# Expert outputs weighted on their way out of PSUM and added to the residual in memory by accumulating scatters

## The reference, cut to what matters

```python
h = h + mix
h = h + hierarchical_moe(rms_norm(h, ffn_norm[i]), ...)
...
# in hierarchical_moe: 32 experts, 2 for each token
weights = g_p * e_p / jnp.sum(e_p, axis=-1, keepdims=True)
return (jax.nn.silu(xb @ w_gate[e]) * (xb @ w_up[e])) @ w_down[e]
y = jax.ops.segment_sum(y_buf[dest] * sw[:, None].astype(y_buf.dtype), st, num_segments=T)
...
return rms_norm(h, final_norm)[:, N_META:]
```

## Time and profile before

| | |
|---|---|
| Time, 3 runs | 3458.29 us median (3456.8 to 3461.87) |
| The profiled execution: its own time, its span | 3462.14 us, 3460.2 us |
| Mean granted TensorE clock | 0.952 |
| PE, DVE, ACT, POOL busy | 3136.4, 1756.7, 1247.0, 1798.2 us |
| Moved by DMA | 536.24 MB, 155 GB/s in the mean |
| Expert stages | about 870 to 1365 and 2860 to 3380 us |
| Projection of layer 1 | about 1371 to 1650 us |
| Last stage | about 3384 to 3460.2 us |

### The profile page before, as it was taken

One profiled execution on the slowest core, in us unless ns is written; L12 is line 12 of the kernel. 1 busy time (PEld: TensorE's weight loads), 2 busy tenths in 40 slices (PEclk: granted clock), 3 DMA queues, 4 the chain that ended last, 5 costly groups with the idle time before them and its releaser, 6 DMA issues. The chain is left out here.

```text
span 3460.2 us, 57020 instructions
## 1 busy us (share of the span) xinstructions
PE 3136.4 (91%) x19621; PEld 2480.0 (72%) x19621; DVE 1756.7 (51%) x4064; ACT 1247.0 (36%) x2675; POOL 1798.2 (52%) x1447
## 2 busy tenths in 40 slices
PE   6999999899699996899799999999997996999990
PEld 4788886687688885799566666666665885888880
DVE  3555555577343332666455555555543663433337
ACT  2444444322122222444344444444443221232222
POOL 2655554244344442345588888888872222444433
PEclk8999999899799998899799999999998997999995
DMA  2001100844788893787502220222004546999957
GB/s 103 27 27 40 40 31 28 261 150 136 259 299 303 304 316 119 240 268 237 150 10 53 53 53 10 53 53 53 10 13 173 183 139 224 347 307 321 308 200 298
DMA packets 360887, 536.24 MB, mean 155 GB/s; under 512 B 82934, under 2 KB 280970, under 8 KB 354169
## 3 DMA queue, kind: packets, MB, share of 16 engines
q1 hardware_dynamic: 333624, 457.43, 41.3%
q0 software_dynamic: 27072, 76.40, 5.7%
HBM read 397.42 MB, written 145.06 MB: 157 GB/s over the span
## 5 line engine op out<-in xcount | busy, mean ns | idle before, releaser
L2148 POOL TENSOR_TENSOR ab_acc<-ab_acc,ab_pT 128x1024 f32<-128x1024 f32 (+2 forms) x320 | 593.9, 1856 | 91.9 <-ACT ab_pT L2182 51.4
L2182 ACT ACTIVATE ab_pT<-ab_S 128x512 f32<-128x512 f32 (+4 forms) x704 | 350.4, 505 | 514.3 <-PE ab_S L2273 244.9
L2205 DVE TENSOR_REDUCE ab_mx<-ab_W 128x2 f32<-128x800 f32 (+1 forms) x224 | 249.8, 1117 | 216.7 <-PE ab_W L2287 212.2
L1303 POOL DMA_INDIRECT scratch_y<-ex_y,ex_prow x65 | 66.0, 1015 | 498.3 <-issue 352.9
L1475 PE MATMUL ex_U<-ex_xT,ex_wu 128*128 128x160 f32 x2080 | 293.1, 299 | 0.0
L1475 PEld LDWEIGHTS ex_U<-ex_xT,ex_wu 128*128 128x128 f32 x2080 | 286.1, 190 | 0.0
L2271 PE MATMUL ab_S<-ab_q_hi,ab_k_hi 97*128 97x512 f32 (+4 forms) x704 | 275.1, 391 | 4.7 <-ACT ab_pT L2182 2.8
L2320 PE MATMUL ab_O<-ab_pT,ab_v 128*64 128x512 f32 (+3 forms) x1280 | 261.7, 547 | 0.0
L2272 PE MATMUL ab_S<-ab_q_lo,ab_k_hi 96*128 96x512 f32 (+4 forms) x704 | 254.3, 361 | 0.0
L2273 PE MATMUL ab_S<-ab_q_hi,ab_k_lo 96*128 96x512 f32 (+4 forms) x704 | 252.5, 359 | 0.0
L1087 PE MATMUL pr_PR<-pr_wo_hi,pr_o_hi 128*128 128x512 f32 x528 | 217.7, 412 | 37.6 <-DVE pr_wo_lo L954 32.6
(11 more groups left out here) (302 smaller groups left out, 7460.2 us busy)
## 6 DMA issues: line engine op xcount, KB each, us to landing
ex_wu<-in_moe_w_up SPq DMA_DIRECT2D x65, 1024.0 KB
ex_wd<-in_moe_w_down SPq DMA_DIRECT2D x65, 1024.0 KB
keep_wg<-in_moe_w_gate SPq DMA_DIRECT2D x33, 1024.0 KB
ring_wg<-in_moe_w_gate SPq DMA_DIRECT2D x32, 1024.0 KB
pb_y<-scratch_y SPq DMA_DIRECT2D x17, 1024.0 KB
pr_o<-scratch_oT SPq DMA_DIRECT2D x33, 512.0 KB
scratch_h<-pr_h SPq DMA_DIRECT2D x33, 512.0 KB, 5.2
scratch_xn<-pr_xn SPq DMA_DIRECT2D x33, 512.0 KB, 2.7
```

What stands on the lines that cost most here:

```text
L2148: nc.gpsimd.tensor_tensor(to, to, pT[:, U % RING, :, 0:n], ALU.add).then_inc(added, 1)
L2182: nc.scalar.activation(pT[:, U % RING, h, 0:n], S[:, h, 0:n], ACT.Exp, scale=B_SCALE).then_inc(exped, 1)
L2205: nc.vector.reduce_max(mx[:, :, t, c:c + 1].rearrange("p h a -> p (h a)"), W[:, j % 2, :, 0:n], AX.X).then_inc(emptied, 1)
```

## The change

Each place of an expert's list now carries the token's row and the bits of its weight instead of a row of y. `find_places` makes the scatter's rows from the token's row, and copies the weight into a new tile `share` with one more instruction. The three copies of Y out of PSUM multiply by that weight. Both scatters of an expert go to `scratch_h` with `compute_op=ALU.add`: the DMA adds to the rows in memory. As two experts can have the same token, GpSimd waits before the scatters of an expert until those of the expert before have landed. The rare extra blocks (`expert_block`) are changed in the same way. `scratch_y`, its zeros, the 16 residual loads during layer 1's experts, and both combining steps are gone: the projection of layer 1 (now `project_b`) and `finish` load `h` alone, and `project_b` no longer stores it. `finish` issues its 16 loads at once. The diff, cut:

```diff
-                    nc.vector.tensor_copy(rowi[:, j.slot, :, :].rearrange("p k a -> p (k a)"), about[:, 3:7])
+                    nc.vector.tensor_copy(rowi[:, j.slot, :, 0], about[:, 3:5])
+                    nc.vector.tensor_copy(rowi[:, j.slot, :, 1].bitcast(F32),
+                                          keep["weights"][:, skip:NT, :][:, tile_at(j), :].rearrange("p a k -> p (a k)"))
...
-                    if layer == 1 and (e.c in (2, 3, 4, 5) if e.turn is None else e.c == 6):
-                        t = (e.c + 4) if e.turn is None else e.turn
-                        at = slice(t, t + 1) if e.turn is None else bass.ds(t, 1)
-                        sp.dma_start(keep["h"][:, at, :].rearrange("p a d -> p (a d)"),
-                                     dram["h"][P:ROWS, :].rearrange("(t p) d -> t p d", p=P)[at, :, :].rearrange("a p d -> (a p) d")
-                                     ).then_inc(keep["h_in"], 16)
...
+                        d = f.back(1)
+                        if f.after(1):
+                            pool.wait_ge(y_out[d.slot], (d.uses + 1) * 32)
                         pool.sem_inc(held, 1)
-                        pool.indirect_dma_start(dram["y"], bass.IndirectOffsetOnAxis(ap=prow[:, f.slot4, 0:1], axis=0),
-                                                y[:, f.slot, :], None, bounds_check=2 * ROWS - 1, oob_is_err=False).then_inc(y_out[f.slot], 16)
-                        pool.indirect_dma_start(y_parts, bass.IndirectOffsetOnAxis(ap=prow[:, f.slot4, 1:2], axis=0),
-                                                yr[:, f.slot, :], None, bounds_check=QN * 2 * ROWS - 1, oob_is_err=False).then_inc(y_out[f.slot], 16)
+                        pool.indirect_dma_start(dram["h"], bass.IndirectOffsetOnAxis(ap=prow[:, f.slot4, 0:1], axis=0),
+                                                y[:, f.slot, :], None, bounds_check=ROWS - 1, oob_is_err=False,
+                                                compute_op=ALU.add).then_inc(y_out[f.slot], 16)
+                        pool.indirect_dma_start(h_parts, bass.IndirectOffsetOnAxis(ap=prow[:, f.slot4, 1:2], axis=0),
+                                                yr[:, f.slot, :], None, bounds_check=QN * ROWS - 1, oob_is_err=False,
+                                                compute_op=ALU.add).then_inc(y_out[f.slot], 16)
...
-                        nc.scalar.copy(y[:, g.slot, 0:512], Y[:, g.c % 2, :]).then_inc(y_act, 1)
+                        act.wait_ge(listed, g.count(1, 1))
+                        nc.scalar.activation(y[:, g.slot, 0:512], Y[:, g.c % 2, :], ACT.Copy, scale=share[:, g.slot4, 0:1]).then_inc(y_act, 1)
                         act.wait_ge(downed, g.count(3, 3))
-                        nc.scalar.copy(yr[:, g.slot, :], Y[:, g.c % 2, 0:QD4]).then_inc(y_act, 1)
+                        nc.scalar.activation(yr[:, g.slot, :], Y[:, g.c % 2, 0:QD4], ACT.Copy, scale=share[:, g.slot4, 1:2]).then_inc(y_act, 1)
...
-                    nc.vector.tensor_scalar(prow[:, e.slot4, 1:2], slot[:, e.slot4, 1, 1:2], float(QN), quarter[:, :], ALU.mult, ALU.add)
-                    nc.vector.tensor_copy(prow[:, e.slot4, 0:1], slot[:, e.slot4, 0, 1:2])
+                    nc.vector.tensor_scalar(prow[:, e.slot4, 1:2], slot[:, e.slot4, 1, 0:1], float(QN), quarter[:, :], ALU.mult, ALU.add)
+                    nc.vector.tensor_copy(prow[:, e.slot4, 0:1], slot[:, e.slot4, 0, 0:1])
+                    nc.vector.tensor_copy(share[:, e.slot4, :], slot[:, e.slot4, :, 1].bitcast(F32))
                     dve.drain().then_inc(listed, 1)
...
-                        nc.vector.tensor_copy(y[:, g.slot, 512:D], Y[:, (1 + g.c) % 2, :]).then_inc(y_dve, 1)
+                        nc.vector.tensor_scalar(y[:, g.slot, 512:D], Y[:, (1 + g.c) % 2, :], share[:, g.slot4, 0:1], None, ALU.mult).then_inc(y_dve, 1)
...
                         sp.wait_ge(xn_ready, i.back(2).count(1, 1))
-                        sp.wait_ge(h_out[i.slot], i.uses * 16)
                     sp.dma_start(h[:, i.slot, :], rows(dram["h"], i)).then_inc(h_in[i.slot], 16)
-                    sp.dma_start(y[:, i.slot, :, :].rearrange("p k d -> p (k d)"),
-                                 rows(dram["y"].rearrange("(r k) d -> r (k d)", k=2), i)).then_inc(y_in[i.slot], 16)
...
-                    if i.live():
-                        sp.wait_ge(summed, i.count(1, 1))
-                        sp.dma_start(rows(dram["h"], i), h[:, i.slot, :]).then_inc(h_out[i.slot], 16)
...
-                        act.wait_ge(summed, h_next.count(1, 1))
+                        act.wait_ge(h_in[h_next.slot], (h_next.uses + 1) * 16)
                         nc.scalar.activation(hsq[:, :], h[:, h_next.slot, :], ACT.Square, accum_out=ssq[:, h_next.slot:h_next.slot + 1])
...
-                    dve.wait_ge(y_in[i.slot], (i.uses + 1) * 16)
-                    for k in range(2):
-                        w = keep["weights"][:, :, k][:, tile_at(i)]
-                        nc.vector.scalar_tensor_tensor(out=h[:, i.slot, :], in0=y[:, i.slot, k, :], scalar=w, in1=h[:, i.slot, :],
-                                                       op0=ALU.mult, op1=ALU.add)
-                        if k == 0:
-                            dve.drain()
-                    dve.drain().then_inc(summed, 1)
...
-                def load(t):
-                    sp.dma_start(y[:, t % DEEP, :, :].rearrange("p k d -> p (k d)"),
-                                 dram["y"].rearrange("(r k) d -> r (k d)", k=2)[P * (t + 1):P * (t + 2), :]).then_inc(y_in[t % DEEP], 16)
-
-                def store(t):
+                for t in range(NB):
+                    sp.dma_start(h[:, t, :], dram["h"][P * (t + 1):P * (t + 2), :]).then_inc(h_in[t], 16)
+                    if t == 0:
+                        sp.dma_start(gain[:, :], bcast(io["final_norm"], D)).then_inc(consts, 16)
...
+                for t in range(NB):
                     sp.wait_ge(xn_ready, t + 1)
                     sp.dma_start(out[P * t:P * t + P, :], xn[:, t % 8, :]).then_inc(xn_out[t % 8], 16)
...
-                    act.wait_ge(summed, t + 1)
-                    nc.scalar.activation(hsq[:, :], residual(t), ACT.Square, accum_out=ssq[:, t:t + 1])
+                    act.wait_ge(h_in[t], 16)
+                    nc.scalar.activation(hsq[:, :], h[:, t, :], ACT.Square, accum_out=ssq[:, t:t + 1])
...
+                dve.wait_ge(consts, 16)
+                for t in range(NB):
                     dve.wait_ge(rstd_ready, t + 1)
-                    if t == 0:
-                        dve.wait_ge(consts, 16)
                     if t >= 8:
                         dve.wait_ge(xn_out[t % 8], 16 * (t // 8))
-                    nc.vector.scalar_tensor_tensor(out=xn[:, t % 8, :], in0=residual(t), scalar=rstd[:, t:t + 1], in1=gain[:, :],
+                    nc.vector.scalar_tensor_tensor(out=xn[:, t % 8, :], in0=h[:, t, :], scalar=rstd[:, t:t + 1], in1=gain[:, :],
                                                    op0=ALU.mult, op1=ALU.mult).then_inc(xn_ready, 1)
-
-                for t in range(NB + 1):
-                    if t < NB:
-                        combine(t)
-                    if t >= 1:
-                        scale(t - 1)
...
```

More of the change, by code:

```diff
@@ L713, in project_and_route @@
         res = s.sb("res", [P, 2, D])
[L714 removed]
+        info = s.sb("info", [P, NT, 5])
         h = s.sb("h", [P, 2, D])
@@ L756, in project_and_route @@
         w_high, w_split = s.sem("w_high"), s.sem("w_split")
-        NCLEAR = 4 if first else 1
+        NCLEAR = 2 if first else 1
         zeroed = s.sem("zeroed")
@@ L1169, in experts @@
         prow = s.sb("prow", [P, 4, 2], I32)
+        share = s.sb("share", [P, 4, 2])
         x = s.sb("x", [P, 4, D])
@@ L1217, in _ @@
                 extra = keep["extra"]
-                def spare(t):
-                    k = t - EARLY
-                    return EXPERTS - 3 + k // 2, late_tile(keep, t)
                 def slots_of(e):
@@ L1272, in _ @@
                 over_steps(sp, 0, 1 + N, 6, EXPERTS - 2, step, unroll=4)
-                for t in range(EARLY, NT - 1) if layer == 1 else ():
-                    e, at = spare(t)
-                    sp.wait_ge(gated, e + 1)
-                    sp.dma_start(at, dram["h"][P * (t + 1):P * (t + 2), :]).then_inc(keep["late_in"], 16)
             @block.gpsimd
@@ L1499, in _, with project_b @@
                 over_steps(pe, 0, 2 + N, 4, EXPERTS, step, unroll=4)
-def combine_and_project_b(nc, io, dram, keep):
+def project_b(nc, io, dram):
     with ExitStack() as ctx:
@@ L2374, in expert_block @@
         y = s.sb("y", [P, D])
+        share = s.sb("share", [P, 1])
         T = s.ps("T", [P, 2, 512])
@@ L2412, in _ @@
                 nc.scalar.activation(act_g[:, :, :].rearrange("p c t -> p (c t)"), G[:, 0:FC * P], ACT.Silu).then_inc(silued, 1)
+                act.wait_ge(shared, 1)
                 act.wait_ge(downed, 1)
-                nc.scalar.copy(y[:, 0:512], Y[:, 0, :]).then_inc(y_ready, 1)
```

(24 more changed lines are left out.)

60 lines of the change are left out of this document (12 added, 48 removed).

## The result

The changed kernel takes 3476.1 us at the median (3468.4 to 3483.4, 10 runs) where the kernel before took 3459.4 beside it (3452.8 to 3462.6, 10 runs): a ratio of **1.0049**, 95% interval 1.0037 to 1.0061. It is slower by some 17 us; the forecast was 3426 us, faster by 32. The profiled execution took 3475.1 us with a span of 3473.2, against 3462.1 and 3460.2.

What follows compares the result with a forecast made beforehand. TensorE was taken to set the pace in expert stages and projection, DMA close behind. Terms -29 - 8 + 3 + 3 - 1 = -32 against the profiled 3462.1 gave 3430, or 3426 us against the median; range 3415 to 3540.

Steps and rivals of the forecast that it cites:

- Expert stages, DMA: Expert steps: accumulating reads delay the scatter's landing by 1.5 us, costing 0.05 us a step, +3 us (0 to +230).
- L: Expert steps: time from a scatter's issue to its landing, read as 9.0 us, forecast 10.5, with up to 10.45 free.
- R1: Expert steps: accumulate lands somewhat later, row writes or reads waiting; L 11.2, +40 instead of +3, 3463 us; chance 0.20.
- R2: GpSimd in expert steps: second scatter meets VectorE's split, lands 1.8 us later; +104 instead of +3, 3527 us; chance 0.22.
- R3: Expert steps: each row takes two turns between the weights' packets; +230 instead of +3, 3653 us; chance 0.12.
- R4: Last stage at 338 GB/s as stores and loads wait; projection gains only the DMA's 3 us; 3441 us; chance 0.08.
- Last stage: Final combining stage: multiply-adds and y loads go, DMA becomes the limit, ending at 3431 instead of 3460.2; -29 us.
- Projection: Start of layer 1's projection: without y loads and multiply-adds, normalisation and first matmul come 8 us earlier; -8 us.
- The experts' computation: Expert stages, compute: copies of Y become multiplications in the same engines and shapes; no difference taken.
- GpSimd's wait: Expert steps: new wait for the scatter before needs landing within 14.3 us; nothing moves unless L passes 13.
- The ends of the expert stages: Last scatters, for which TensorE waits: +1.5 us each for the second read, +3 us (0 to +6).
- The routing: Routing: one more small copy of weights a tile, 33 times 0.15 us, beside a busy TensorE; costs nothing.

## Why the prediction was wrong

**The step that failed** is *Expert stages, DMA*: "L = 9.0 + 1.5 = 10.5, against 10.45 free. Step cost 0.05 us, 57 steps, +3 us". That a longer landing closes a loop over VectorE was right, and the runs show it. Both numbers of the step were wrong: L was 11.0, and 10.45 was not free everywhere.

- *The cost.* I added the bytes of the read and nothing on GpSimd. An adding scatter takes GpSimd 1.6 us, not 1.0, and both are issued one after the other, so 1.2 us were due there alone. The landing behind it, which I priced at 1.5, gave 0.4 to 0.7 in the steps.
- *The free time.* The 10.45 were read from one step (3049.86) and used for 57. In the 41 steps without `list_beyond` the loop is L + 3.6, so 10.7 were free. In the 14 with its instruction of 1.2 us it is L + 4.84, so only 9.4 were, and even the L of the forecast would have cost 1.1 us a step there. No term of the sum had this work.

The product of the forecast, with the measured L, gives (11.0 - 10.45) x 57 = +31, near the measured 36. That is luck: it charges 0.55 us to each step, where the 41 lost 0.26 and the 14 lost 1.77, less the lag that is free. The run in which only the large one adds shows the difference: a mean L of 10.4, below 10.45, and 12 us lost, 11 of them in the four steps a layer at the end of those with `list_beyond`. No run takes `list_beyond` out of the loop, so its share of the loss is worked out from the steps' times and not measured by itself.

The 5.1 us of the scatter at 1311.26 were not "with no weights in flight". The last load of down weights, 1 MB, was issued at 1309.86, and the DMA engines were at a share near 1 from 1312 to 1315. So the 4.0 us of queueing in the upper bound of the term stand on nothing; no run shows this scatter alone.

**The rivals.** R1 comes nearest by its numbers: L 11.2 for 11.0, a step of 15.0 for 15.18, +40 for +36. The nearness of the last two is partly luck, as above, and its cause, reads that wait or queue, covers at most the 0.4 to 0.7 us of later landing; the larger part was GpSimd's own time, which no rival had alone. It had a chance of 0.20 because I looked for a delay in the DMA only. R2 had the right mechanism mostly at the wrong place: the first scatter met the split in 15 of 57 steps and took 3.7 us, while the second was held up by some 0.3 us in most of the others and by 1.6 in two (3.2 us at the most). It did not decide, since colliding steps have an L only 0.4 us longer than the others: in them the landing comes 5.8 us after the second scatter's end instead of 7.1, so a good part of the extra time on GpSimd lies beside the landing of what was already issued. By the Trainium skill (SBUF — State Buffer, "Who interferes with whom") a `tensor_tensor` doesn't hold up descriptor generation, which the page marks as inferred. The scatter of 3.66 us at 1054.95, beside a split from 1054.84 of 2.28 us, where others take 1.61, speaks against it again. The same section of the Trainium skill has a VectorE instruction with two SBUF inputs, as the split is, contend with a GpSimd instruction that reads SBUF, so "this could not be" said more than the page does. No run here shows which access holds the scatter up. R3 (two turns a row, +230) did not come. R4 did not either: the last stage runs at 420 GB/s from 3432 to 3468.

**The terms that held.** Last stage -26.9 for -29: 360 GB/s over the whole of it, with 217 until 3432 and 139 from 3468, where the first loads and the last stores stand alone. Projection -6.4 for -8 from load to last matmul, with the first matmul 8.7 us behind the first load where it was 16.3 (I had called it moved by 8 us: 7.6). The experts' computation nothing, as the run with two writing scatters shows (steps 441.9 and 479.9). GpSimd's wait nothing, by its control. The ends of the expert stages +6.7 for +3, or 3.3 each for 1.5: from the last large scatter's issue to the next stage's first load it is 12.2 and 11.3 us instead of 8.9 and 8.0. GpSimd's time for the two, undisturbed, is 1.1 us of each, and 2.1 us lie behind it: with no weights in flight the adding scatters land that much later. The routing +4 for nothing; its cause is not the extra copy that I had priced at nothing, and is open.

The sum against the result: +33 from the steps, +4 from the ends, +4 from the routing, and +4 from the last stage, the projection and the small rest make 45 us, from -32 to +13. The result lies in the range (3415 to 3540), not by the forecast's own (3415 to 3440) but as R1 and R2 had widened it, and on the side to which I gave 0.42.

## What to carry to other kernels

A wait of 221 us that costs nothing is a debt: before lengthening what it waits for, compute how much longer it may be in every kind of step, those with extra work behind the wait above all, and not from one step or a mean. Count the issuing engine's own time as well as the transfer's. Where the slack is under a microsecond, move the wait first: asking for the landing one step later turned a loss of 0.5% into a gain of 0.65%. And an experiment that changes numbers can change the path through a program that branches on them; compare such runs by their stages.
